# A hybrid streaming layer on 8 cores: from an order written by hand to one made by a list scheduler at build time

## The reference

```python
h = rms_norm(x, g1)
g_b, g_c, x_a, x_l, g_l = split(h @ w_in)              # 5 x 512 columns
out_a = g_b * conv3_causal(g_c * x_a)                  # mixer A
xc = conv4_causal(x_l) + b
r, i = sigmoid(blockdiag(xc, wa) + ba), sigmoid(blockdiag(xc, wx) + bx)
a = exp(-8 * r * softplus(a_param))
b_t = sqrt(1 - a*a) * (i * xc)                         # first frame of a prompt: factor 1
h_t = a_t * h_(t-1) + b_t                              # recurrence over the frames
out_b = h_t * gelu(g_l)                                # mixer B
x = x + concat(out_a, out_b) @ w_out
x = x + square(relu(rms_norm(x, g2) @ w_up)) @ w_down  # hidden width 4096
y = rms_norm(x, gf)
```

## Time and profile before

| | us |
|---|---|
| median of 3 runs | 1123.35 |
| lowest and highest | 1122.01, 1127.64 |
| span of the profiled execution, slowest core (core 0) | 1136.6 |
| TensorE busy | 863.3 (76%) |
| VectorE, ScalarE, GpSimd busy | 487.4, 468.7, 321.0 |
| DMA moved by the core | 213.81 MB, 188 GB/s |

### The profile page before, as it was taken

One profiled execution on the slowest core, in us unless ns is written; L12 is line 12 of the kernel. 1 busy time (PEld: TensorE's weight loads), 2 busy tenths in 40 slices (PEclk: granted clock), 3 DMA queues, 4 the chain that ended last, 5 costly groups with the idle time before them and its releaser, 6 DMA issues.

```text
span 1136.6 us, 15917 instructions; the slowest of 8 cores (1105.4 to 1136.6 us)
## 1 busy us (share of the span) xinstructions
PE 863.3 (76%) x4213; PEld 410.3 (36%) x4213; DVE 487.4 (43%) x692; ACT 468.7 (41%) x816; POOL 321.0 (28%) x424
## 2 busy tenths in 40 slices
PE   0153254266479679996999997999999799994995
PEld 0121121122134234443444443444444345551752
DVE  0366786766342103736313547323436421435201
ACT  0447966857025213363531545341535341443211
POOL 5134644647005311121220212121224121112210
PEclk9986665688689979998999999899999899997787
DMA  8978799999437998776458777457787347985681
GB/s 200 151 127 137 160 144 180 141 178 131 84 130 126 134 255 282 217 238 231 140 148 254 236 234 260 129 148 220 245 245 254 115 147 215 296 286 179 216 252 61
DMA packets 152655, 213.81 MB, mean 188 GB/s; under 512 B 66694, under 2 KB 66754, under 8 KB 151928
## 3 DMA queue, kind: packets, MB, share of 16 engines
q1 hardware_dynamic: 93072, 178.36, 50.7%
q0 software_dynamic: 57952, 33.56, 22.4%
q10 hardware_dynamic: 1544, 0.87, 0.4%
HBM read 227.36 MB, written 33.62 MB: 230 GB/s over the span
## 4 chain that ended last, share of the span: by engine, by line
PE 61%; DMA 11%; ACT 11%; DVE 9%; issue 6%; ACTq 1%; POOL 0%; DVEq 0%; POOLq 0%; SPq 0%
PE ps L717 21%; PE ps L755 19%; PE ps L454 12%; DMA sb_ring<-wscr 8%; ACT sb_t_rig L273 5%; PE ps L731 3%; ACT sb_hb L273 2%; DMA sb_t_rig<-wx 2%; ACT sb_t_om L273 2%; PE ps L438 2%; PE ps L688 2%; DVE sb_t_xc_c L285 1%; DVE sb_hb L280 1%; DVE sb_xsl L276 1%; DVE sb_hTb L276 1%
## 5 line engine op out<-in xcount | busy, mean ns | idle before, releaser
L717 PE MATMUL ps<-sb_hTb,sb_ring 128*128 128x512 bf16 (+1 forms) x1280 | 269.4, 375 | 24.4 <-DMA sb_ring<-wscr 16.7
L755 PE MATMUL ps<-sb_ring,sb_uT 128*128 128x512 bf16 x1024 | 225.6, 379 | 0.0
L454 PE MATMUL ps<-sb_hTa,sb_ring 128*128 128x512 bf16 (+1 forms) x864 | 193.8, 384 | 41.2 <-DMA sb_ring<-wscr 36.0
L717 PEld LDWEIGHTS ps<-sb_hTb,sb_ring 128*128 128x128 bf16 x1280 | 129.7, 102 | 157.0 <-issue 39.8
L273 ACT ACTIVATE sb_rl<-ps 128x512 bf16<-128x512 f32 (+1 forms) x160 | 88.7, 555 | 201.0 <-PE ps L717 201.0
L276 POOL TENSOR_TENSOR sb_uT<-sb_rl 128x512 bf16<-128x512 bf16 (+1 forms) x80 | 76.4, 955 | 306.4 <-ACT sb_rl L273 294.4
L755 PEld LDWEIGHTS ps<-sb_ring,sb_uT 128*128 128x128 bf16 x1024 | 100.2, 98 | 119.5
L454 PEld LDWEIGHTS ps<-sb_hTa,sb_ring 128*128 128x128 bf16 x864 | 88.1, 103 | 143.2 <-issue 69.4
L438 PE MATMUL ps<-sb_identb,sb_hb 128*128 128x128 bf16 x416 | 41.8, 261 | 107.7 <-DVE sb_hb L280 106.7
L273 ACT ACTIVATE sb_hb<-sb_xsl 128x1024 bf16<-128x1024 f32 x70 | 73.3, 1047 | 121.2 <-DVE sb_xsl L276 111.1
L276 DVE TENSOR_TENSOR sb_uT<-sb_rl 128x512 bf16<-128x512 bf16 (+1 forms) x80 | 31.8, 398 | 201.0 <-ACT sb_rl L273 200.9
(11 more groups left out here) (111 smaller groups left out, 922.5 us busy)
## 6 DMA issues: line engine op xcount, KB each, us to landing
sb_ring<-wscr SPq DMA_DIRECT2D x612, 256.0 KB, 3.8
sb_xsl<-xl SPq DMA_DIRECT2D x16, 512.0 KB, 7.5
sb_xsl<-xp SPq DMA_DIRECT2D x16, 512.0 KB, 5.2
wscr<-w_up POOLq DMA_DIRECT2D x32, 256.0 KB, 12.4
wscr<-w_down POOLq DMA_DIRECT2D x32, 256.0 KB, 29.9
yp<-sb_xsl POOLq DMA_DIRECT2D x16, 512.0 KB, 3.5
wscr<-w_in POOLq DMA_DIRECT2D x20, 256.0 KB, 33.9
wscr<-w_out POOLq DMA_DIRECT2D x8, 256.0 KB, 7.1
```

The lines of the kernel that those rows point to most:

```text
L454: S.group("pe", [lambda e, kc=kc, slot=slot, b=b: e.matmul(out=bank_ap(b, N), lhsT=slot[:, kc * 128:(kc + 1) * 128], rhs=hTs[hi][:, kc * 5 ...
L717: S.group("pe", [lambda e, kc=kc, slot=slot, b=b: e.matmul(out=bank_ap(b, N), lhsT=slot[:, kc * 128:(kc + 1) * 128], rhs=hTs[1][:, kc * 51 ...
L755: fns.append(lambda e, kc=kc, j=j, jj=jj, half=half, slot=slot: e.matmul(out=bank_ap(2 * jj + half), lhsT=uT[:, kc * 512 + j * 128:kc * 51 ...
```

## The change

- **Order.** Every tile's work is written as generators ("strands") that ask for buffers and hand over one operation at a time with an assumed duration. `Weaver.run` picks, at build time, the ready operation with the earliest possible start on its engine, then by priority, and appends it to the engines' lists. Engines still run in order with semaphores; only the order differs. A ring load is placed with the matmul group that uses it. Assumed are 0.08 us for a hand-off between engines, 5.0 us per MB for GpSimd's DMAs (0.52 MB each, one behind the other) and 0.85 us for a weight load, each channel by itself.
- **Tiles.** The order of first norms and mixers is L0, S, L1, L2, L3, M0 to M3. The MLPs run S, M0, M1, M2, M3, each starting once the one before has issued its last matmul. Mixers and projections of the next tile have better priority than an MLP and go in wherever they are ready and hold buffers.
- **Weights.** The host lays out all of w_in, w_up and w_down as contiguous blocks (`wall`, 84 of them) and w_out as one [128, 8192] array. `g_conv` (lowest priority) issues all 84 conversions and two for w_out, which now goes to SBUF in bf16 and stays. The pool of semaphores lets 48 be outstanding. The ring has 12 slots instead of 15.
- **Buffers.** Three transposed norm buffers instead of two, three sets for mixer B instead of two, one for mixer A, own mixer outputs for S. Convolution history is kept in small halo tiles. x is loaded by ScalarE's queue instead of SP's.
- **Parameters** come packed in one array; state outputs are stored without transposes, in a layout that the host turns round.

The durations and the arithmetic of the single operations are the same but for small things (the sqrt works in the buffer of r, the scan writes over xc). The core of the diff:

```diff
-R = 15
-OC_ORDER = [12, 16, 13, 17, 14, 18, 15, 19, 0, 4, 8, 1, 5, 9, 2, 6, 10, 3, 7, 11]
-POS_OF_OC = {oc: i for i, oc in enumerate(OC_ORDER)}
-CH_OUT, CH_UP, CH_DOWN, NCHUNK = 20, 28, 60, 92
+R = 12
+CH_UP, CH_DOWN, NCHUNK = 20, 52, 84
...
+    def _start(self, r):
+        kind = r[0]
+        if kind == "op":
+            _, eng, dur, fns, rd_, wr_, ring = r
+            st = self.t[eng]
+            lat = self.LAT if eng != "pe" else 0.0
+            for b in rd_:
+                st = max(st, b.tw + self.LAT)
+            for b in wr_:
+                st = max(st, b.tw + lat, b.tr + self.LAT)
+            if ring is not None:
+                slot_b, scr, issue, land = self._ring_times(ring)
+                st = max(st, land + self.LAT)
+            return st
+        _, q, out, in_, rd_, wr_, pool, mb, kw = r
+        st = self.t[q]
+        for b in rd_:
+            st = max(st, b.tw + self.LAT)
+        for b in wr_:
+            st = max(st, b.tw + self.LAT, b.tr + self.LAT)
+        return st
...
+    def _ring_times(self, ring):
+        slot_b, scr = ring["peek"]()
+        scr = ring["scr"]
+        issue = max(self.t["sp"], slot_b.tw, slot_b.tr + self.LAT, scr.tw + self.LAT) + 0.06
+        land = max(issue + 2.0, self.t["hw"]) + 0.85
+        return slot_b, scr, issue, land
...
+            self.S.dma(q, out, in_, rd_, wr_, pool, **kw)
+            ch = "sw" if q == "pool" else "hx"
+            self.t[q] = st + (0.6 if q == "pool" else 0.06)
+            land = max(self.t[q] + 2.0, self.t[ch]) + mb * (5.0 if q == "pool" else 3.4)
+            self.t[ch] = land
...
+    def run(self):
+        self._settle()
+        while self.ready:
+            best, bk = None, None
+            for s in self.ready:
+                st = self._start(s.req)
+                k = (st, s.prio, s.seq)
+                if bk is None or k < bk:
+                    best, bk = s, k
+            self.ready.remove(best)
+            self._emit(best, bk[0])
+            self._advance(best, None)
+            self._settle()
...
+    wall = din("wall", [NCHUNK, 128, 1024])
+    wout_d = din("wout", [128, 8 * 1024])
+    par_d = din("par", [128, PAR_COLS])
+    wbd_d = din("wbd", [128, 8 * 128])
...
+        P_x, P_hb, P_hT, P_T, P_A = Slots(range(8)), Slots(range(2)), Slots(range(NHT)), Slots(range(NT)), Slots(range(1))
+        P_bank, P_rl, P_stat = Slots(range(8)), Slots(range(3)), Slots(range(6))
...
+        def PER(dur, mk, rd_, wr_, chunk):
+            def load():
+                s_ = rstate["i"] % R
+                rstate["i"] += 1
+                ap = ring[:, s_ * 1024:(s_ + 1) * 1024]
+                S.dma("sp", ap, wscr[chunk], [scr_b[chunk]], [ring_b[s_]], "ring")
+                return ap, ring_b[s_]
+            return ("op", "pe", dur, mk, rd_, wr_,
+                    {"peek": lambda: (ring_b[rstate["i"] % R], None), "scr": scr_b[chunk], "load": load})
...
+        def g_conv(order):
+            for chunk in order:
+                yield DMA("pool", wscr[chunk], wall[chunk], [], [scr_b[chunk]], "cv", 0.52)
+                if chunk == 15:
+                    yield DMA("pool", wbd[:], wbd_d, [], [wbd_b], "par", 0.5)
+                if chunk == 19:
+                    for hf in range(2):
+                        yield DMA("pool", wout[:, hf * 4096:(hf + 1) * 4096], wout_d[:, hf * 4096:(hf + 1) * 4096], [],
+                                  [wout_b], "cv", 2.1)
...
+        Ss = mk_tile("S", "S", xs, 0, 256, 4, 6, ys, 0)
+        chain = Ls[0:1] + [Ss] + Ls[1:] + Ms
...
+        def g_xloads():
+            for t in chain:
+                if t is Ms[0]:
+                    yield tok("h1L3", 2)
+                for j in range(t.J):
+                    k, = yield get(P_x)
+                    yield DMA("act", xap(k), t.src[t.row0 + j * 128:t.row0 + (j + 1) * 128, :], [], [xsl_b[k]], "x", 0.52)
+                    t.xs[j] = k
+                    W.mark("x" + t.name)
...
+        def g_norm1s():
+            yield tok("set0")
+            yield tok("par")
+            for ti, t in enumerate(chain):
+                if t in Ms and t is not Ms[0]:
+                    yield tok("h2got" + chain[ti - 1].name)
+                (t.h1,) = yield get(P_hT)
+                for j in range(t.J):
+                    yield tok("x" + t.name, j + 1)
+                    W.spawn(g_norm(t, j, g1t, t.h1, "h1" + t.name, t.lean), t.prio)
+                t.nproj = 4 if t.lean else 20
+                W.spawn(g_hfree(t), t.prio)
+                W.mark("h1on" + t.name)
...
+        def g_mbs():
+            for ti, t in enumerate(chain):
+                yield tok("h1" + t.name, t.J)
+                for c in range(4):
+                    (q,) = yield get(P_T)
+                    W.spawn(g_mb(t, c, q), t.prio)
+
+        def g_mas():
+            for t in [Ss] + Ms:
+                yield tok("h1" + t.name, t.J)
+                for c in range(4):
+                    (q,) = yield get(P_A)
+                    W.spawn(g_ma(t, c, q), t.prio + 1)
...
+            yield CP("dve", 0.68 * f, xb3[:, :, 3:3 + L], v3(bank_ap(b, N), Sq), [bank_b[b]], [xbb])
+            W.put(P_bank, [b])
+            xc = T["xc"][:, 0:N]
+            xc3 = v3(xc, Sq)
+            yield TS("dve", 0.6 * f, xc3, xb3[:, :, 0:L], lcw[:, c:c + 1], lcb[:, c:c + 1], ALU.mult, ALU.add, [xbb, par_b], [T["b_xc"]])
+            for kk in range(1, 4):
+                yield STT(0.82 * f, xc3, xb3[:, :, kk:kk + L], lcw[:, 4 * kk + c:4 * kk + c + 1], xc3, ALU.mult, ALU.add,
+                          [xbb, par_b, T["b_xc"]], [T["b_xc"]])
+            yield CP("dve", 0.42, T["xcb"][:, 0:N], xc, [T["b_xc"]], [T["b_xcb"]])
...
+        def g_out(t):
+            yield tok("mix" + t.name, 8)
+            (t.h2,) = yield get(P_hT)
+            W.mark("h2got" + t.name)
+            for j in range(t.J):
+                bs = yield get(P_bank, 2)
+                for g in range(4):
+                    yield PE(4 * 0.217, [lambda e, kc=kc, half=half, b=b, j=j: e.matmul(
+                        out=bank_ap(b), lhsT=t.mix[:, kc * t.N + j * 128:kc * t.N + (j + 1) * 128],
+                        rhs=wout[:, kc * 1024 + half * 512:kc * 1024 + (half + 1) * 512], start=(kc == 0), stop=(kc == 7))
+                        for kc in (2 * g, 2 * g + 1) for half, b in enumerate(bs)], list(t.mix_b) + [wout_b], [bank_b[b] for b in bs])
+                W.spawn(g_res(t, j, bs), t.prio)
...
+        def g_mlp(t, prev, prio, keep):
+            yield tok("h2" + t.name, t.J)
+            if prev is not None:
+                yield tok("mlp" + prev.name)
+            N = t.N
+            h2 = hTs[t.h2]
             for fc in range(32):
-                if mid_hook is not None and 8 <= fc <= 16 and fc % 2 == 0:
-                    mid_hook((fc - 8) // 2)
-                slot, sbuf_ = ring_load(CH_UP + fc)
-                b = nextbank()
-                S.group("pe", [lambda e, kc=kc, slot=slot, b=b: e.matmul(
-                    out=bank_ap(b, N), lhsT=slot[:, kc * 128:(kc + 1) * 128], rhs=hTs[1][:, kc * 512:kc * 512 + N],
-                    start=(kc == 0), stop=(kc == 7)) for kc in range(8)], [sbuf_, hT_bs[1]], [bank_b[b]])
-                k = st["rl"] % 2
-                st["rl"] += 1
-                rl_ap = rl[:, k * 512:k * 512 + N]
-                act(rl_ap, bank_ap(b, N), AF.Relu, [bank_b[b]], [rl_b[k]])
-                tt("dve" if fc % 2 == 0 else "pool", uT[:, fc * 512:fc * 512 + N], rl_ap, rl_ap, ALU.mult, [rl_b[k]], [uT_b[fc]])
...
+                    yield PER(4 * 0.217, lambda slot, kc=kc, bs=bs, js=js: [
+                        lambda e, jj=jj, j=j, half=half: e.matmul(
+                            out=bank_ap(bs[2 * jj + half]), lhsT=uT[:, kc * 512 + j * 128:kc * 512 + (j + 1) * 128],
+                            rhs=slot[:, half * 512:(half + 1) * 512], start=(kc == 0), stop=(kc == 31))
+                        for jj, j in enumerate(js) for half in range(2)], [uT_b[kc]], [bank_b[b] for b in bs], CH_DOWN + kc)
+                for jj, j in enumerate(js):
+                    W.spawn(g_epi(t, j, bs[2 * jj:2 * jj + 2]), t.prio + 8)
+            W.mark("mlp" + t.name)
...
+        order = [12, 13, 14, 15] + [16, 8, 4, 0, 17, 9, 5, 1, 18, 10, 6, 2, 3, 7, 11, 19] + list(range(CH_UP, NCHUNK))
+        W.spawn(g_setup(), -20)
+        W.spawn(g_conv(order), 500)
+        W.spawn(g_par(), -19)
+        W.spawn(g_xloads(), -10)
+        W.spawn(g_norm1s(), -1)
+        W.spawn(g_mbs(), -1)
+        W.spawn(g_mas(), -1)
+        W.spawn(g_halo_a(), 10)
+        prev = None
+        for t in [Ss] + Ms:
+            W.spawn(g_out(t), t.prio)
+            W.spawn(g_mlp(t, prev, 0, 0), 100 if t is Ss else 101 + int(t.name[1]))
+            prev = t
+        W.spawn(g_state("S", soT_s, soT_s_b, sts_d), 90)
+        W.spawn(g_state("M3", soT_p, soT_p_b, stp_d), 90)
+        W.run()
...
```

(20 more changed lines are left out.)

1080 lines of the change are left out of this document (470 added, 610 removed).

## The result

The changed kernel takes 1145.94 us (median of 4 executions, 1142.81 to 1150.86) against 1123.8 of the kernel before beside it: ratio 1.0187, 95% interval [1.0145, 1.0228]. It is slower by 1.9%, where 1020 us was forecast.

A forecast was written before the change was run, and what follows sets the result against it. TensorE was taken as the bound from 425 us on, with no engine full in the state-only tiles. 400 to M0's MLP + 616 + 20 = 1036 us, less 13: 1023, rounded to 1020; own range 965 to 1060, all cases 915 to 1085.

The forecast's parts named there:

- What bounds the kernel: State-only tiles: no engine full; first main tile: waits for weights of 35.9 and 43.1 us; from 425 us: TensorE.
- the starvation: Front: conversions hold the software queue above 80%, other queues under 20%, loads landing after over 20 us.
- E: End of the weight conversions: 221 us for 92 chunks, 20 for x tiles, 5 of start, about 246 us.
- T: Start of M0's MLP, after conversions and the remaining front work: 246 + 155, about 400 us.
- T - E: Front after the conversions: VectorE's 144 us at 0.93, so 155 us, with the small tile's MLP hidden inside.
- Main tiles, 604 + 20: From M0's MLP on: MLPs 436 us, fronts of M1 to M3 168, plus 20 for down passes and fixed order.
- Middle stage worse: Rival: down passes wait and fixed order costs, end 1075, or small tile's MLP uncovered, 1078; chance 0.17.
- Mild starvation: Rival: x loads starve less, front bound by VectorE's whole work, T 276, end 899; chance 0.22.
- The fixed order breaks up TensorE's stream: Rival: main tiles' 64 groups of transposes and gates wait 2.1 us each, 134 us, end 1142; chance 0.06.
- Parameters, w_out, x loads on ScalarE's queue: Packed parameters gain up to 25 us at the front, counted as nothing; w_out's loads already hide; x loads cost nothing.
- Part 1's aside: Weight conversions: contiguous form costs 2.4 us a chunk against 3.0 strided, but squeezes the other queues harder.

The follow-up runs named there:

- experiment 2: Changed kernel with rows of the bf16 weights in HBM padded by 128 bytes, so conversions go in short packets: 1080.39 us, ratio 0.9596.
- experiment 7: Kernel before with only the rows of its bf16 weights in HBM padded, 64 elements further apart: 1109.49 us, ratio 0.9869.
- experiment 3: Changed kernel with all 84 conversions and w_out's two DMAs at the head of GpSimd's queue: 1145.33 us, ratio 1.0189.
- Experiment 4: Changed kernel with all conversions at the head of GpSimd's queue, but behind the set-up's memsets: 1141.88 us, no ratio.
- experiment 10: Changed kernel, long packets kept, with the 256-token tile put back to the end: 1148.56 us, ratio 1.0221.
- Experiment 8: Changed kernel with padded rows (short packets) and longer x load and store times in the build-time model: 1048.9 us, ratio 0.933.
- experiment 6: Kernel before with all 92 blocks of the weights contiguous, its order and pace untouched: 1135.21 us, ratio 1.0096.

## Why the prediction was wrong, step by step

- **What bounds the kernel, and the starvation: right.** From 150 to 250 us the software queue is over 80% (88.4, 86.9) and the other two under 20%, with one load per 11 us, landings far over 20 us and TensorE about half busy at most. Experiments 2 and 7 show the cause, packets of unlike size taking equal turns.
- **E, the conversions' end (246, measured 312): wrong by its first assumption.** "As fast as it takes them" overlooked that GpSimd's queue is in order and that the scheduler put L0's products between the conversions, timed by a model with no starvation. The software queue works 0 to 78 us, rests to 130 and works to 312: 52 us of pause, and 260 us of work where the sum had 246, which leaves 14 to its terms. But experiments 3 and 4 took the pause away, and T moved by 6 us. So an earlier end of the conversions did not bring an earlier T: the pause was at the same time the tiles' only good stretch. Both experiments also held GpSimd until about 110 us, so it stays open what the pause alone cost. For the same reason the state forecast at 246 us (L0, the small tile's mixers and L1 done) came true by luck. Experiment 4 has the conversions without the long pause, as the sum meant them, and at 248 us only L0 and the small tile are done: beside conversions that run all the time, and with GpSimd held at the start, less gets done than I had counted.
- **T - E, 155 us (measured 166, and 202 in experiments 3 and 4): a near hit by a wrong sum, and the step that failed most.** I summed VectorE, 144 us, and put the small tile's MLP at nil beneath it, "55 without that cover". In 350 to 478 us TensorE was the full engine, 118 of 129 us, and by experiment 10 the whole tile costs 83 us before M0's up, where the sum has only its 18 us of VectorE (a part of the 83 arises before 312 us, from its loads among the conversions). I had summed one engine and never TensorE over the same stretch. This step was the costliest: with short packets too the tile costs as much in the front (109) as at the end (101), and the gain that I booked by dropping most of the old last 115 us was not there.
- **Main tiles, 604 + 20 (measured 651): mechanism named, size missed.** TensorE's rate is right (M0's up runs at 22.61 us for 104 matmuls, of which the row has 102). The 3 us a tile for the fixed order and 2 for the down pass, 20 in all, measure 651 - 604 = 47. Of these 29 are one chain: store of y, x load, norm, transposes, with transfers of 9 and 10 us for 4.6 and 3.8. For weights TensorE never waits after 478 us, so the down pass's share is nil. I had read x loads beside weight loads only as bandwidth, not as latency in TensorE's in-order queue. Experiment 8 gets 30 us back by the model's numbers alone. The periods were 184, 185 and 172 us for the 170 asked.
- **The rivals.** "Middle stage worse" had two right mechanisms, the fixed order and the uncovered small tile, in its cases of 1075 and 1078, one by one and not together (its waits of the down passes did not come), and held no case with T beyond 460. "Mild starvation" is refuted: even without conversions the front is 323. "The fixed order breaks up TensorE's stream" was the one slower case. It came true in kind but small: 29.4 us in 7 waits at transposes and 5.1 in 3 at gates after 478 us, not 134 in 64. That its end of 1142 lies beside the measured 1146 is luck. The slower sign came from elsewhere, from three mis-sized terms of one direction that I had let vary one at a time.
- **Parameters, w_out, x loads on ScalarE's queue: nothing of the miss was traced to them.** None was tried by itself.
- **Part 1's aside that the contiguous form is cheaper per chunk but squeezes harder** is borne out where it can be read (2.4 to 2.5 us a chunk in long packets, 3.1 in the short ones of experiment 2, which are not the strided form), and experiment 6 shows which wins: the kernel before is 1% slower with it.

What stays open: how the 323 us of front without conversions are made up (TensorE is busy 216 of them and waits 56 for normed x and 32 for VectorE's convolution); the 82 of the 156 us of starvation that short packets leave, which bandwidth and the loads' waits for conversions share in a way no run separates; what the pause cost with GpSimd free; and whether the small tile could be hidden with a front cut for it. With TensorE busy 461 of 500 us in the main part, its 77 to 109 us have little room there.

## What to carry to other kernels

When a background stream of DMAs runs beside loads that are waited for, compare the packet counts and bytes of the queues: equal counts with unequal bytes mean here that the long packets set the pace of the others, and shortening them (here by a padded row) can be worth more than making them efficient. A build-time order is only as good as the transfer times in its model; give it those that the trace shows under load, above all where a load waits for a store. And before booking a moved piece of work at nil, add up the engine that it needs over the stretch where it goes, after everything else there has been moved too.

## What the runs showed of the hardware

- Rows of 2 KB that lie end to end in HBM went in the software queue as packets of some 16 KB with about as many short ones (8.2 KB in the mean); with 128 bytes between them the mean was 1.8 KB. Queues that ran side by side had packet counts within 1% of each other: 633 and 638, 1132 and 1131, 2245 and 2247, and three of them 545, 547 and 548. In 200 to 250 us of experiment 2 the counts were 2325 and 2119.
- DMA busy 1.00 at 128 GB/s (150 to 200 us) and 0.61 at 182 GB/s (500 to 1000 us): the busy share says nothing of what is moved.
- A store of 512 KB took 9 us and a load of 512 KB 10 beside weight loads (medians 8.3 and 8.9 from 500 to 1000 us), where a weight load of half the size lands in 3.8 among its like the earlier trace rows.
- Sixty-four DMAs handed to GpSimd in a row took 30.9 us to issue, 0.48 each.
